# The last expert round moved into the next program block, and both halves of its down product put ahead of its spread

## The chip, the cores and the metric

The kernel runs on one core of a Trainium2 chip. The time is that of one launch in microseconds on the device, from the first to the last instruction and the little that lies around them. The core has a tensor engine (PE in the profile), a vector engine (DVE), a scalar engine (ACT), GpSimd (POOL) and SyncE (SP), which here only issues transfers. Engines run on their own instruction streams and meet through semaphores.

## What is computed

A two-layer step on 256 prompt tokens and 8 sample tokens, width 1024, all in float32. Layer 0 mixes by retention, layer 1 by gated linear attention (GLA); each is followed by a mixture of 64 experts, of which every token uses 8, plus a shared one. Cut to what matters here:

```python
for i in range(DEPTH):
    mod = silu(c) @ ada_w[i] + ada_b[i]                 # conditioning: shifts, scales, gates
    h = modulate(x, norm_mix_g[i], sh1, sc1)            # rmsnorm, scale, shift
    m, S = retention_mixer(h, ...) if i % 2 == 0 else gla_mixer(h, ...)
    x = x + g1[:, None, :] * m
    h = modulate(x, norm_ffn_g[i], sh2, sc2)
    f = moe_ffn(h, ...)      # routed: sum of w * (silu(h Wg[e]) * (h Wu[e])) Wd[e]; plus shared
    x = x + g2[:, None, :] * f
return rmsnorm(x, final_norm_g), ...
```

## The kernel before, in words

The token state is held transposed, `k.x` as 8 chunks of 128 features by 264 tokens. The kernel is a row of program blocks (`nc.Block()`): `retention`, `experts(k, 0)`, `gla`, `experts(k, 1)`, `final`. In a block each of the five engines has its own function. At the end of a block each engine drains and waits at a barrier for all five; only then does any of them start the next block.

`experts` has two blocks. In the first the 64 experts are gone through in 16 rounds of four. Weights come through a ring of 12 slots of 1 MB (`k.ring`), a round filling it once: four gate, four up, four down matrices. SP issues each load when the slot's last reader has released it (`ring_free`). Most rounds run on PE as gate and up products, the spread of the round before (`spread`: its result rows are multiplied into token columns, 8 chunks, two PSUM banks in turn), transposes of the hidden rows, the gather of the next round's rows and the down product. Each spread chunk is added on DVE to `acc` (`add_spread`, L2799).

The last two rounds, `LAST - 1` and `LAST`, are light: one tile with 32 rows for each expert. Round `LAST` in order: gate (`four_up`, L2337), spread of round `LAST - 1` (L2395), up (L2337), hidden on DVE (L2836) and its transpose (L2411), copied by ACT (L2994); the down product's first half (`four_down`, L2347), copied to `last_rows` by ACT (L3013). Meanwhile DVE adds all of `acc`, gated, to `k.x` (`add_last`, three instructions for each chunk, L2806 to L2811). `last_spread` (L2367) then spreads chunks 0 to 3 (L2380), computes the down product's second half, and spreads chunks 4 to 7. Each of these chunks goes to `k.x` by `add_last`. The down matrices of this round are loaded in halves of columns (L2252, 8 transfers of 512 KB), the first halves under a semaphore of their own.

Behind the spread, in the same block: for layer 0 the next norm (`nxt`: squares on ACT L505, sums over features on PE L524, reciprocal root, then `k.h` chunk by chunk on DVE L552 and ACT L516) and a product for the next conditioning (L457); for layer 1 the transposes back to token rows (L1912) and the final norm's sums (L1920, L1928).

The second block of `experts` holds a loop for token rows that fit in none of the 16 rounds. Every engine loads the number of such pairs (L3062, L3097 and the like) and branches over the loop when it is zero, as it is for these inputs. Then `gla` or `final` begins. The first product of `gla` (`project`, L1361) reads `k.h`, all of which is ready by the barrier; its small gate weights `a1`, `a2` are the first thing SP loads there (L1316). After the last round SP has loaded six slots for the next stage (four of conditioning weights, two of `gla_w_in`); the other slots are loaded from the next block.

## Time and profile before

| | us |
|---|---|
| median of 3 runs | 1618.62 |
| lowest, highest | 1614.11, 1620.0 |
| the profiled execution | 1614.77 |
| its span, first to last instruction | 1613.0 |
| PE busy | 1516.2 (94%) |
| DVE busy, ACT busy | 709.3 (44%), 364.3 (23%) |

The span is cut at the places of interest by instruction times counted from its start. Rows of an engine with a q behind its name (PEldq, SPq) are those of its sequencer: branches, drains, register loads, DMA issues. A number in square brackets with an arrow says how long the engine was idle before the group and what ended it. The last round of layer 0 begins near 866 us and the GLA block at 909.5 us; the last round of layer 1 begins near 1574 us and the final block at 1605.4 us.

### The profile page before, as it was taken

How to read it: one execution, taken by the hardware profiler on the slowest of the kernel's cores; microseconds unless marked ns; L12 is line 12 of the kernel's file. 1: busy time of each engine (PE TensorE's matmuls, PEld its weight loads, DVE VectorE, ACT ScalarE, POOL GpSimd, SP SyncE). 2: the span in 40 equal slices, each digit the busy share in tenths (PEclk: the TensorE clock that was granted, in tenths of full speed). 3: DMA queues.
4: the chain of work that ended last, by engine and by line, in shares of the span. 5: the costliest groups of instructions: out<-in, count | busy, mean ns of one | idle time of the engine just before them, and what ended most of it. 6: DMA issues, size and time to landing. Idle time of an engine off the chain costs nothing. (4 is left out here: it accounts for less than half of the span.)

```text
span 1613.0 us, 29632 instructions
## 1 busy us (share of the span) xinstructions
PE 1516.2 (94%) x11206; PEld 1009.5 (63%) x11206; DVE 709.3 (44%) x1980; ACT 364.3 (23%) x770; POOL 94.0 (6%) x119
## 2 busy tenths in 40 slices
PE   6999999998999999999997799999999999999986
PEld 4778765776665665565554487767566556565553
DVE  3205535215465355345454235443745534543453
ACT  3002443103111121112111244431111111211112
POOL 0000110001000000000000000001000000010000
PEclk9999999999999999999999899999999999999998
DMA  9997799339999999999999793988999999999896
GB/s 364 388 370 266 259 394 404 124 98 367 393 420 420 420 421 420 419 420 419 398 370 409 265 291 110 351 305 325 420 420 421 421 420 420 420 419 410 338 420 248
DMA packets 153578, 580.21 MB, mean 360 GB/s; under 512 B 17181, under 2 KB 62401, under 8 KB 105226
## 3 DMA queue, kind: packets, MB, share of 16 engines
q1 hardware_dynamic: 137642, 535.74, 83.8%
q0 software_dynamic: 15200, 40.92, 6.6%
q10 hardware_dynamic: 640, 2.26, 0.4%
q8 instruction: 61, 1.00, 0.3%
q14 instruction: 35, 0.29, 0.0%
HBM read 567.17 MB, written 26.90 MB: 368 GB/s over the span
## 5 line engine op out<-in xcount | busy, mean ns | idle before, releaser
L2431 PE MATMUL ps<-ring,scratch 128*64 128x256 f32 x3328 | 367.8, 380 | 10.0 <-DMA ring<-in_moe_w_up 8.8
L2431 PEld LDWEIGHTS ps<-ring,scratch 128*64 128x64 f32 x3328 | 245.0, 137 | 121.6 <-issue 14.3
L2497 PE MATMUL ps<-ring,scratch 128*64 128x512 f32 x896 | 200.5, 598 | 0.0
L698 PE MATMUL ps<-hT,ring 128*128 128x264 f32 x768 | 182.5, 392 | 1.3 <-ACT hT L380 1.3
L2836 DVE SCALAR_TENSOR_TENSOR scratch<-scratch,ps 128x256 f32<-128x256 f32 x62 | 29.8, 481 | 327.4 <-ACT scratch L2985 313.4
L2395 PE MATMUL ps<-scratch 128*128 128x264 bf16 x1392 | 169.6, 276 | 1.5 <-DVE scratch L2803 1.5
L698 PEld LDWEIGHTS ps<-hT,ring 128*128 128x128 f32 x768 | 147.6, 194 | 31.4 <-issue 2.8
L2395 PEld LDWEIGHTS ps<-scratch 128*128 128x128 bf16 x1392 | 121.8, 97 | 50.2 <-issue 14.3
L2803 DVE TENSOR_TENSOR scratch<-scratch,ps 128x264 f32<-128x264 f32 x240 | 102.6, 430 | 86.3 <-PE ps L2395 86.0
L2497 PEld LDWEIGHTS ps<-ring,scratch 128*64 128x64 f32 x896 | 58.1, 136 | 117.7 <-issue 86.2
L2985 ACT ACTIVATE scratch<-ps 128x256 f32<-128x256 f32 x62 | 23.8, 384 | 424.6 <-PE ps L2431 356.3
L2164 POOL DMA_INDIRECT scratch<-h_rows,scratch x60 | 59.8, 997 | 897.9 <-DVE scratch L2158 889.3
L3015 ACT CAST scratch<-ps 128x512 bf16<-128x512 f32 x116 | 68.0, 586 | 145.2 <-PE ps L2497 139.9
L1361 PE MATMUL ps<-hT,ring 128*128 128x264 f32 x384 | 91.9, 396 | 9.5 <-PEq L3059 9.5
L2897 DVE TENSOR_TENSOR scratch<-ps,scratch 128x512 f32<-128x512 f32 x116 | 79.7, 687 | 25.9 <-ACT scratch L3015 25.9
L1361 PEld LDWEIGHTS ps<-hT,ring 128*128 128x128 f32 x384 | 74.1, 196 | 23.4 <-issue 10.3
L2887 DVE TENSOR_TENSOR scratch<-scratch 128x512 bf16<-128x512 f32 x116 | 80.4, 693 | 4.0
L2311 PE MATMUL ps<-tab,scratch 128*128 128x128 f32 x480 | 65.1, 279 | 13.0 <-DVE scratch L2631 9.7
L2311 PEld LDWEIGHTS ps<-tab,scratch 128*128 128x128 f32 x480 | 51.8, 141 | 24.7 <-DVE scratch L2631 16.4
L955 DVE SCALAR_TENSOR_TENSOR ring<-ring,rstd 128x512 f32<-128x512 f32 x64 | 41.3, 687 | 49.7 <-ACT rstd L1108 36.7
L2631 DVE COPY scratch<-ps 128x512 f32<-128x512 f32 x60 | 41.5, 692 | 48.5 <-PE ps L2311 48.5
L859 PE MATMUL ps<-scratch,ring 128*128 128x264 f32 x256 | 57.7, 387 | 0.0
(402 smaller groups left out, 1458.3 us busy)
## 6 DMA issues: line engine op xcount, KB each, us to landing
ring<-in_moe_w_gate SPq DMA_DIRECT2D x128, 1024.0 KB, 20.1
ring<-in_moe_w_up SPq DMA_DIRECT2D x128, 1024.0 KB, 21.9
ring<-in_moe_w_down SPq DMA_DIRECT2D x120, 1024.0 KB, 18.0
ring<-in_ada_w SPq DMA_DIRECT2D x48, 1024.0 KB, 12.4
ring<-in_ret_w_in SPq DMA_DIRECT2D x24, 1024.0 KB, 16.7
ring<-in_state_ret SPq DMA_DIRECT2D x16, 1024.0 KB, 14.0
out_ret_sample<-ring POOLq DMA_DIRECT2D x16, 1024.0 KB, 9.2
ring<-in_gla_w_in SPq DMA_DIRECT2D x12, 1024.0 KB, 12.0
```

Source lines behind the costliest of these rows:

```text
L698: mm = nc.tensor.matmul(k.ps[:, bank, 0:T], w[:, c, m * P:(m + 1) * P], k.h[:, c, :], start=(c == 0), stop=(c == DC - 1))
L859: mm = nc.tensor.matmul(k.ps[:, out_bank(n), 0:T], w[:, c, m * P:(m + 1) * P], vo[:, 4 * h + c, :], start=(h == 0 and c == 0), stop=(h == ...
L1361: mm = nc.tensor.matmul(k.ps[:, bank, 0:T], w[:, c, m * P:(m + 1) * P], k.h[:, c, :], start=(c == 0), stop=(c == DC - 1))
L2164: pool.indirect_dma_start(xtok_of(p), None, h_rows[:, :], bass.IndirectOffsetOnAxis(ap=rows[:, p:p + 1], axis=0), bounds_check=ABSENT - 1, ...
L2311: mm = nc.tensor.transpose(k.ps[:, b, c * P:(c + 1) * P], xtok_of(p)[:, d0:d0 + P], ident)
L2395: mm = nc.tensor.matmul(k.ps[:, c % 2, 0:T], parts_of(p)[:, s, c * P:(c + 1) * P], slot_token[:, p, :], start=(p == 0 and s == 0), stop=(p ...
L2431: mm = nc.tensor.matmul(k.ps[lo:lo + CAP, 2 + p, j * DE:(j + 1) * DE], xg[:, p, c, lo:lo + CAP], slot(k, n, DE)[:, c, :], start=(c == 0), ...
L2497: mm = nc.tensor.matmul(k.ps[lo:lo + CAP, 6 + half, :], hid_t[:, p, m, lo:lo + CAP], slot(k, n, D)[:, m, half * 512:(half + 1) * 512], sta ...
L2803: nc.vector.tensor_tensor(acc[:, c, :], acc[:, c, :], k.ps[:, c % 2, 0:T], ALU.add).then_inc(s_add, 1)
L2887: nc.vector.tensor_tensor(parts_of(p)[:, 2, cols], rest[:, half], parts_of(p)[:, 1, cols], ALU.subtract).then_inc(s_part, 1)
L2897: nc.vector.tensor_tensor(rest[:, half], k.ps[:, 6 + half, :], parts_of(p)[:, 0, cols], ALU.subtract).then_inc(s_rest, 1)
L3015: nc.scalar.copy(parts_of(p)[:, 0, cols], k.ps[:, 6 + half, :]).then_inc(s_rhi, 1)
```

## The change

Four things are done.

1. Round `LAST` leaves the first block of `experts`. That block now ends behind round `LAST - 1`. For SP it still holds all loads of round `LAST`. At its end each engine waits for the count of extra pairs and loads it (`read_pairs`).
2. The second block is gone. `experts` returns an object with one function for each engine (`tail_tensor` and so on), and `gla` and `final` call these at the head of their own block. Each holds an `If` on the number of extra pairs, whose body has round `LAST` and the loop for the extra rows, and an `Else` with round `LAST` alone; behind both come the next norm and the conditioning product, or the final sums, and then the block's own work. What was ordered by a barrier is now ordered by semaphores: the first `project` waits for each chunk of `k.h`, `a1` is loaded when the norm's sums are done (they share memory), `final` waits for the sums.
3. In `last_spread` both halves of the down product come ahead of all eight chunks.
4. On DVE the gated addition of `acc` to `k.x` moves from round `LAST` to round `LAST - 1`, ahead of that round's hidden rows; the spread of round `LAST - 1`, done in round `LAST`, now goes to `k.x` by `add_last` and no longer to `acc`.

Beside these, SP loads all 12 slots for the next stage as they come free, and GpSimd clears old semaphores at the end of `gla` and no longer at its start.

```diff
+    def read_pairs(eng, name):
+        eng.wait_ge(s_count, 2)
+        extra_pairs[name] = eng.value_load(number, min_val=0, max_val=XPAIRS)
...
-            k.issued = n_end
-            load_until(k, sp, n_end + KEPT)
-            for i in range(KEPT):
-                sp.wait_ge(k.ring_free[(n_end + KEPT + i) % RING], (n_end + KEPT + i) // RING)
-            sp.wait_ge(s_count, 2)
-            with sp.If(sp.value_load(number, min_val=0, max_val=XPAIRS) > 0):
-                load_extra(sp, X_LOADS, pair_experts(sp, 0))
+            read_pairs(sp, "sp")
...
-        def last_spread(pe, behind):
+        def last_spread(pe, follow):
             d = done_tiles(LAST, 0)
             pe.wait_ge(s_htc, LAST + 1)
+            wait_light(pe, LAST, "moe_w_down")
+            four_down(0, LIGHT_BLOCKS, 1, LIGHT_PLACE)
             for half in range(2):
-                if half:
-                    wait_light(pe, LAST, "moe_w_down")
-                    four_down(0, LIGHT_BLOCKS, 1, LIGHT_PLACE)
-                    behind(pe, 0)
-                    behind(pe, 1)
                 pe.wait_ge(s_part, 2 * d + 1 + half)
                 for c in range(4 * half, 4 * half + 4):
                     pe.wait_ge(s_add, DC * (LAST + 1) + c - 1)
                     nc.tensor.matmul(k.ps[:, c % 2, 0:T], last_rows[:, c * P:(c + 1) * P], last_token,
                                      start=True, stop=True).then_inc(s_scat, 1)
-                    if half:
-                        behind(pe, c - 2)
+                    if c >= 2 and follow:
+                        follow(pe, c - 2)
...
-            for r in range(HEAVY - 2, LAST + 1):
+            for r in range(HEAVY - 2, LAST):
                 pe_round(pe, r)
-            last_spread(pe, x_rows if layer else nxt.sum)
...
+            read_pairs(pe, "pe")
...
+            if last:
+                for c in range(DC):
+                    v.wait_ge(s_scat, DC * (r - 1) + c + 1)
+                    add_last(v, c, k.ps[:, c % 2, 0:T], DC + c).then_inc(s_add, 1)
+            elif light(r):
+                add_spread(v, r - 1)
+                v.wait_ge(s_add, DC * (r + 1))
+                for c in range(DC):
+                    ins = add_last(v, c, acc[:, c, :], c)
+                k.dve.link(v, ins)
...
-    with nc.Block() as block:
...
+    def tail_sync(sp):
+        k.issued = n_end
+        load_until(k, sp, n_end + KEPT)
+        pairs = extra_pairs["sp"]
+        with sp.If(pairs > 0):
+            ...
+        load_until(k, sp, n_end + RING)
...
+    def tail_tensor(pe):
+        ...
+        with pe.If(pairs > 0):
+            pe_round(pe, LAST)
+            last_spread(pe, None)
+            ...
+        with pe.Else():
+            pe_round(pe, LAST)
+            last_spread(pe, follow)
+            for c in range(DC - 2, DC):
+                follow(pe, c)
+        if layer:
+            pe.wait_ge(s_final, 3)
+            final_small(k, pe, small).then_inc(s_final, 1)
+        else:
+            cond_products(k, pe, k.ps[:, 4], next_group)
...
-def gla(k):
+def gla(k, behind):
...
         @block.sync
         def _(sp):
+            behind.sync(sp)
+            sp.wait_ge(behind.norm.s_sum, 1)
             sp.dma_start(a1, inp["gla_w_a1"][0].rearrange("(c p) r -> p c r", p=P)).then_inc(s_w, 16)
...
+            behind.tensor(pe)
...
+                    if first:
+                        pe.wait_ge(behind.norm.s_h, c + 1)
...
 def final(k, behind):
...
+            behind.vector(v)
+            v.wait_ge(behind.s_sums, 2)
+            v.wait_ge(behind.s_final, 4)
```

On PE, in layer 0 where round `LAST - 1` ends with its down product (32x512), the order before goes straight on to the gate product of round `LAST` (32x256):

```order
L2347 MATMUL ps<-ring,scratch 32x512 [waits ring_full9,ring_full8,ring_full10,ring_full7,moe0_hidden_transposed_out]
L2347 MATMUL ps<-ring,scratch 32x512 x15
L2337 MATMUL ps<-ring,scratch 32x256 [waits ring_full0,ring_full1,ring_full11,ring_full2,moe0_gathered_out_odd,moe0_gathered_out_even]
L2337 MATMUL ps<-ring,scratch 32x256 x31
L2395 MATMUL ps<-scratch 128x264 [waits moe0_added,moe0_row_parts,moe0_slots_first_out]
```

In the changed kernel (its line numbers) this stands there:

```order
L2369 MATMUL ps<-ring,scratch 32x512 [waits ring_full9,ring_full8,ring_full10,ring_full7,moe0_hidden_transposed_out]
L2369 MATMUL ps<-ring,scratch 32x512 x15
L2159 TENSOR_LOAD scratch [waits moe0_listed]
L2159 ISA x2
L2252 UNCONDITIONAL_BRANCH
L1355 UNCONDITIONAL_BRANCH [waits barrier_Pool_Activation_PE_DVE_SP_release]
L3102 COMPARE_AND_BRANCH
```

A load of the count, the barrier and a branch now stand between the two rounds. The branch leads over 80 rows of the order (the `If` body) to the gate product in the `Else` body; before, the branch over the extra loop led over 48 rows.

On SP, in layer 0 where the down matrices of round `LAST` are issued in halves, the order before was:

```order
L2252 DMA ring<-in_moe_w_down 128x2x512
L300 DMA ring<-in_ada_w 128x2x1024 [waits ring_free11]
L300 DMA ring<-in_ada_w 128x2x1024 [waits ring_free0]
L300 DMA ring<-in_ada_w 128x2x1024 [waits ring_free1]
L300 DMA ring<-in_ada_w 128x2x1024 [waits ring_free2]
L300 DMA ring<-in_gla_w_in 128x8x256 [waits ring_free3]
```

In the changed kernel, at the same last half load:

```order
L2279 DMA ring<-in_moe_w_down 128x2x512
L2159 TENSOR_LOAD scratch [waits moe0_listed]
L2159 ISA x2
L2252 UNCONDITIONAL_BRANCH
L1310 UNCONDITIONAL_BRANCH [waits barrier_Pool_Activation_PE_DVE_SP_release]
L299 DMA ring<-in_ada_w 128x2x1024 [waits ring_free11]
```

SP comes to the barrier only behind the last of the eight half loads, and the loads of the next stage are behind the barrier.

On PE, in the last round of layer 0 behind the first half of the down product, the chunks of the spread (L2399) and the norm's sums (L521) now follow one another from the third chunk on:

```order
L2369 MATMUL ps<-ring,scratch 32x512 [waits ring_full9,ring_full8,ring_full10,ring_full7,moe0_slots_first_out]
L2369 MATMUL ps<-ring,scratch 32x512 x7
L2399 MATMUL ps<-scratch 128x264 [waits moe0_added,moe0_row_parts]
L2399 MATMUL ps<-scratch 128x264 [waits moe0_added] x2
L521 MATMUL ps<-scratch,tab 128x264 [waits setup_x_loaded]
L2399 MATMUL ps<-scratch 128x264 [waits moe0_added]
L521 MATMUL ps<-scratch,tab 128x264 [waits setup_x_loaded]
```

Before, four chunks stood ahead of the second half and no sum ahead of it.

## Rows read from the trace of the kernel before

**Rows 1.** Timeline, SP around the last round, layer 0: start, length, line.
```profile
861.73 15.41 SPq L2252 DMA_DIRECT2D ring<-in_moe_w_down  x8
882.34 10.51 SPq L300 DMA_DIRECT2D ring<-in_gla_w_in  x2
```
**Rows 2.** Source line L2252 in that stretch: min, median, max in ns.
```profile
L2252 SPq DMA_DIRECT2D ring<-in_moe_w_down  x8: 544/1133/4172, 861.7 to 876.1; - x8
DMA to landing us min/median/max: 11.1/15.0/17.7
```
**Rows 3.** Source lines at block ends, whole span: load of the count, branches, drain.
```profile
L3062 SPq TENSOR_LOAD <-scratch x2: 263/264/264, 904.3 to 1603.7; - x2
L2225 ACTq DRAIN  x2: 808/1114/1419, 903.3 to 1602.1; - x2
L3098 PEldq COMPARE_BRANCH  x2: 334/2028/3722, 905.4 to 1604.6; - x2
```
**Rows 4.** DMA issues from 846 to 866 us: a gather beside the weight loads.
```profile
scratch<-h_rows,scratch POOLq DMA_INDIRECT x1, 8.6
```
**Rows 5.** Timeline, PE from the last round to the GLA block, layer 0.
```profile
866.58 5.89 PE L2337 MATMUL ps<-ring,scratch 128*32 128x256 f32 x64 [5.33 <-DMA ring<-in_moe_w_gate]
876.53 3.66 PE L2337 MATMUL ps<-ring,scratch 128*32 128x256 f32 x64
881.97 1.92 PE L2347 MATMUL ps<-ring,scratch 128*32 128x512 f32 x16 [0.62 <-DMA ring<-in_moe_w_down]
884.64 1.13 PE L2380 MATMUL ps<-scratch 128*128 128x264 f32 x4 [0.74 <-issue]
886.11 1.25 PE L2380 MATMUL ps<-scratch 128*128 128x264 f32 x4 [0.35 <-DVE xT L2811]
893.12 0.61 PE L2380 MATMUL ps<-scratch 128*128 128x264 f32 x2
894.01 0.61 PE L2380 MATMUL ps<-scratch 128*128 128x264 f32 x2
909.55 10.30 PE L1361 MATMUL ps<-hT,ring 128*128 128x264 f32 x32 [9.46 <-PEq L3059]
923.45 7.39 PE L1361 MATMUL ps<-hT,ring 128*128 128x264 f32 x32
```
**Rows 6.** Timeline, DVE and ACT beside them.
```profile
896.54 0.43 DVE L541 TENSOR_SCALAR scratch<-ps 128x264 f32<-128x264 f32 x1 [1.26 <-PE ps L524]
900.52 3.30 ACT L516 ACTIVATE hT<-hT,mod 128x256 f32<-128x256 f32 x8 [3.04 <-DVE hT L552]
```
**Rows 7.** A window in the gate product: length, PE, PEld, DVE, ACT, POOL busy, clock, DMA.
```profile
868.00:870.00 2.00, 2.00 (x25) 1.02 (x21) 0.00 (x0) 0.00 (x0) 0.00 (x0) 0.50 1.04 434
```
**Rows 8.** Source line L2808, the gated addition of `acc`, from 880 to 886 us.
```profile
L2808 DVE SCALAR_TENSOR_TENSOR xT<-scratch,mod,xT x8: 475/476/480, 880.8 to 884.6; 128x256 f32<-128x256 f32 x8
```
**Rows 9.** Timeline, DVE in round `LAST - 1`, layer 0.
```profile
855.63 0.48 DVE L2836 SCALAR_TENSOR_TENSOR scratch<-scratch,ps 128x256 f32<-128x256 f32 x1 [3.27 <-PE ps L2337]
863.20 0.69 DVE L2887 TENSOR_TENSOR scratch<-scratch 128x512 bf16<-128x512 f32 x1
```
**Rows 10.** Timeline, the last round of layer 1 and the final block.
```profile
1582.38 1.71 SPq L2252 DMA_DIRECT2D ring<-in_moe_w_down  x2
1574.39 5.27 PE L2337 MATMUL ps<-ring,scratch 128*32 128x256 f32 x64 [5.96 <-DMA ring<-in_moe_w_gate]
1584.33 3.66 PE L2337 MATMUL ps<-ring,scratch 128*32 128x256 f32 x64 [0.60 <-DMA ring<-in_moe_w_up]
1589.70 1.93 PE L2347 MATMUL ps<-ring,scratch 128*32 128x512 f32 x16 [0.55 <-ACT scratch L2994]
1600.16 0.61 PE L2380 MATMUL ps<-scratch 128*128 128x264 f32 x2
1603.29 0.20 ACT L1920 ACTIVATION_READ_ACCUMULATOR scratch<-ps 128x1 f32 x1
1605.35 1.28 ACT L1945 ACT_TABLE_LOAD   x1 [1.86 <-PEq L3059]
```

More of the change, by code:

```diff
@@ L191, in build @@
         retention(k)
[L192 to L195 removed]
+        behind = experts(k, 0)
+        gla(k, behind)
+        behind = experts(k, 1)
+        final(k, behind)
 def retire_semaphores(k):
@@ L1463, in _ @@
                     pe.wait_ge(s_qk, 2 * (t - 1))
-                project(t, 0, 2 * (t % 2))
+                if t == 0:
+                    pe.wait_ge(behind.norm.s_samples, 1)
+                project(t, 0, 2 * (t % 2), first=t == 0)
                 project(t, 1, 2 * (t % 2) + 1).then_inc(k.ring_free[loads[t] % RING], 1)
@@ L1927, in final_small, with final @@
     for c in range(DC):
-        k.nc.tensor.matmul(k.ps[0:NS, 0, 0:1], small[:, c, :], k.ones[:, 0:1], start=(c == 0), stop=(c == DC - 1))
-def final(k, sums):
+        mm = k.nc.tensor.matmul(k.ps[0:NS, 0, 0:1], small[:, c, :], k.ones[:, 0:1], start=(c == 0), stop=(c == DC - 1))
+    return mm
+def final(k, behind):
     nc, out = k.nc, k.out
@@ L1937, in final @@
     meansq, root, rstd = (k.scratch[:, (TT + 1) * D + 4 * i:(TT + 1) * D + 4 * i + TT] for i in range(3))
+    sums = behind.sums
     n_gain = k.stage["final_gain"]
@@ L3025, in _ @@
             take(act, 0, 1, nc.scalar.copy, g_odd)
-            round_(0)
+            scalar_round(act, 0)
             with act.Fori(1, HEAVY - 1) as r:
-                round_(r)
-            for r in range(HEAVY - 1, LAST + 1):
-                round_(r)
-            if layer == 0:
-                for c in range(DC):
-                    act.wait_ge(s_add, DC * (LAST + 1) + c + 1)
-                    nxt.square(act, c)
-                nxt.scalar(act)
-                wait_used(k, act, next_group[-1])
-                nc.scalar.copy(next_rows(k), k.ps[:, 4, 0:256])
-            else:
-                nc.scalar.activation(silu[0:1, 0, 0:1], ident[0:1, 0:1], ACT.Sqrt)
-                act.wait_ge(s_final, 1)
-                final_squares(k, 0, sums, junk)
-                act.wait_ge(s_final, 2)
-                nc.scalar.activation(small, k.x[:, :, TP:T], ACT.Square).then_inc(s_final, 1)
-                final_squares(k, 1, sums, junk)
+                scalar_round(act, r)
+            for r in range(HEAVY - 1, LAST):
+                scalar_round(act, r)
+            read_pairs(act, "act")
     release_semaphores(k, old + routed)
@@ L3228, in experts @@
-    return sums
+        tail.s_sums, tail.s_final, tail.sums = k.sem(f"{tag}_final_sums"), s_final, sums
+    else:
+        tail.s_rows, tail.norm = k.sem(f"{tag}_next_mod_rows_out"), nxt
+    def tail_sync(sp):
[3 more added lines that the diff above has]
+        with sp.If(pairs > 0):
+            for i in range(KEPT):
+                sp.wait_ge(k.ring_free[(n_end + KEPT + i) % RING], (n_end + KEPT + i) // RING)
+            load_extra(sp, X_LOADS, pair_experts(sp, 0))
+            with sp.Fori(1, pairs) as i:
+                which_ = pair_experts(sp, i)
+                sp.wait_ge(x_gu, i)
+                load_extra(sp, X_LOADS[0:4], which_)
+                sp.wait_ge(x_dn, 2 * i)
+                load_extra(sp, X_LOADS[4:6], which_)
+            sp.wait_ge(s_final if layer else nxt.s_sum, 2 if layer else 1)
+        load_until(k, sp, n_end + RING)
```

722 lines of the change are left out of this document (356 added, 366 removed).

## The prediction

> **What bounds the kernel now.** The page gives PE 94% of the span, so a change that moves no matmul can only win or lose where PE stands still. I read it in this order. First the waits, for places where PE waits for something other than a result: the longest is 9.46 us ahead of the first GLA product, ended by the barrier behind the extra block [rows 5]. Then the timeline of PE, SP and DVE around the last expert round of each layer, since that is where the change puts its new barrier. The reader is to see two things in it. Round `LAST` of layer 0 starts at 866.58 us, held by the landing of its gate weights for 5.33 us [rows 5]. And SP is at that time in the middle of issuing the eight half loads of the down matrices: the group begins at 861.73 and ends 15.41 us later, at 877.14 [rows 1]. It isn't eight cheap issues: one takes from 0.54 to 4.17 us [rows 2], since the queue is full and SP is held until there is room. The same is seen in the next loads (two `gla_w_in` issues over 10.51 us). In layer 1 the same group ends at 1582.38 + 1.71 = 1584.09, while its gate product began at 1574.39 [rows 10]. Third, the lines at block ends, for what a barrier and a branch cost [rows 3].
>
> **The new barrier, layer 0.** All eight half loads stay in the first block, so the barrier ahead of round `LAST` can't open before 877.14. Behind it:
> - SP loads the count: 0.26 us by the row and some more for its checks and drain, 0.5 in all (an estimate; the load is the only part with a row here) -> 877.6.
> - the barrier. ACT's drain of the first block ended at 903.3 + 0.81 = 904.1 and the first load of the count began on SP at 904.3 and, as the latest, PE's branch at 905.4 [rows 3]. Taken out the load of the count, 0.5 -> 878.1. The count is loaded ahead of the barrier now.
> - PE's branch over the `If` body. One branch of this kind took 0.33 us in layer 1 and 3.72 in layer 0 [rows 3]. The new one leads further, over 80 rows of the order and not 48. I take the long one, 3.7 -> 881.8, and 0.1 to the first matmul.
>
> So the gate product starts at 881.9 and not at 866.58: **+15.3 us**. The 5.33 us that PE had waited for weights are covered by that and are no gain.
>
> In layer 0 the rule of the Trainium skill that bears on the branch is in "Runtime: NRT & Kernel Launch", section Instruction fetch mechanics: a taken branch to a place outside the pages held near the engine must first fetch them by DMA. The two branch times of rows 3 agree in kind: at one and the same line the longer is eleven times the shorter. By that rule the farther branch is the likelier to be long, in both layers; the same page gives PE the largest such memory, 2048 instructions, by which it would be short. The sum goes by the rows, and the short case is a rival below.
>
> **The rest of the round, layer 0.**
> - Gate product. PE has now idled some 19 us. It had idled 5.33 before, which already sufficed: the granted clock from 868 to 870 was 0.50, that is 1.2 GHz [rows 7], and the product took 5.89 us where the same 64 matmuls at 2.4 GHz, of the up weights, took 3.66 [rows 5]: 2.2 us lost. After 9.46 us of idling the GLA product lost 10.30 - 7.39 = 2.9 [rows 5]. I take the 2.9: **+0.7**.
> - Spread of round `LAST - 1`. Eight chunks took from 866.58 + 5.89 to 876.53, 4.1 us. DVE now needs three instructions for each chunk instead of one. The later spread shows the pace with three: a pair of chunks to the next pair 886.11 - 884.64 = 1.47 us [rows 5]. Three such steps and a last pair of 0.85 give 5.3: **+1.2**.
> - Up product to the down product: 876.53 to 881.97, 5.4 us, of which 0.62 waited for the first half of the down weights. ACT and the transposes fill the same time; I leave it at 5.4, **0**. The last half load lands at 876.1 + 11.1 = 887.2 [rows 2], long before PE is there, so neither half of the down product waits for weights.
> - Down product and spread. Before: from 881.97 to the end of the norm's sums at 896.54 [rows 6], 14.5 us, with a stop between the halves of the spread for the second half's copy and the squares queued behind it on ACT. After: two halves back to back 2 x 1.92; the first pair of chunks and its addition 1.5 (the same step of 1.47); from then on a chunk and a sum by turns at 894.01 - 893.12 = 0.89 us, five steps to the start of the last chunk; from there to the end of the sums as before, 896.54 - 894.01 = 2.5. That is 3.85 + 0.1 + 1.5 + 4.45 + 2.75 (0.2 more for a square that ACT starts later) = 12.65: **-1.9**.
>
> The sums end at 896.5 + 15.3 + 0.7 + 1.2 - 1.9 = 911.8.
>
> **The removed block ends, layer 0.** Before, from the end of the sums to the end of the first GLA product (909.55 + 10.30 = 919.85) 23.3 us passed. They were the norm, two barriers with one branch, and a product at half clock. After: the first chunk of `k.h` is out 900.52 + 0.41 + 0.1 - 896.54 = 4.5 us behind the sums [rows 6]. ACT brings one each 3.30 / 8 = 0.41 us and PE reads one in 7.39 / 16 = 0.46, so PE isn't held, and the conditioning product (3.66 us) has kept it busy until just before. 4.5 + 7.4 = 11.9: **-11.4**. Layer 0 in all: 15.3 + 0.7 + 1.2 - 1.9 - 11.4 = **+3.9 us**.
>
> **Loads of GLA.** The slots are released later (gate slots at some 888.4), but all 12 are then loaded as they come free. `a1` now stands in SP's queue behind them. Eight of the 12 MB are issued from 897.5 on, some 20 us of transfers behind the conditioning loads, so `a1` lands around 922 to 924, and it is wanted at 911.8 + 11.9 = 923.7. I take 0.5 us, with 0 and 2.6 as ends. Nothing else waits there.
>
> **The moved addition of `acc`.** In round `LAST - 1` it comes ahead of the hidden rows. Eight chunks go at (884.6 - 880.8) / 7 = 0.54 us [rows 8], 4.4 with the link; DVE idled 3.27 us there [rows 9]. PE gets its hidden rows 1.2 us later and ends the round 1.2 us later. That is covered by the wait for SP until 877.1; were that gone, it would be covered by the 5.33 us wait for weights. The down slots free 1.2 us later as well, which SP's full queue hides.
>
> **Layer 1.** SP ends at 1584.09, so the gate product starts at 1584.09 + 0.5 + 0.5 + 3.7 + 0.1 = 1588.9 instead of 1574.39 [rows 10]: +14.5. Gate: 3.66 + 2.9 = 6.6 where it took 5.27: +1.3. Spread: before it ran from 1579.7 to 1584.33, with 0.60 of waiting for the up weights that are now long there: +0.6. Down, spread, transposes: before, from 1589.70 to the start of the last chunk at 1600.16, 10.5; after 3.95 + 1.5 + 5 steps of 0.78 (the pace of this layer, four chunks in the 3.1 us to 1600.16) = 9.4: -1.0. Block end: the last sum ended at 1603.49 and the root could start at 1605.35 + 1.28 = 1606.63, behind two barriers and a table load; after, the mean square (0.4 us) and a semaphore stand between, and the order holds no table load there: 0.6 for 3.15, -2.55. In all **+12.9 us**.
>
> **The sum**: 3.9 + 0.5 + 12.9 = +17.3 us on the profiled execution's 1614.8: 1632.1. That execution lies 3.9 us below the median of the three runs (1618.6); on the median it would be 1635.9. I forecast the middle, **1634 us**.
>
> **Unknown costs.** The branch: 0.33 us at one end, which takes 3.4 from each layer. At the other end a small transfer that queued beside the weight loads, the gather [rows 4], took 8.6 us; if the code's fetch does too, each layer is 4.9 longer. On DVE and ACT the same branches are hidden by the gate product's 6.6 us. The barrier: between nothing and the 1.3 us from the end of ACT's drain to PE's branch [rows 3].
>
> **Rivals.**
> - The branch is short in both layers. For it: the 0.33 of layer 1. Against: the longer way. 1634 - 6.8 = 1627.
> - The fetch is slow beside the full queue. For it: the gather's 8.6 us, and the loads queued at 877 us land only by 887. Against: nothing shows it for code. 1634 + 9.8 = 1644.
> - `a1` behind the 12 MB costs its upper end and the conditioning loads, issued 11 us later than before, come late too: 3 to 4 us, 1638.
> - SP is not what opens the barrier, the other side: if SP handed its issues to the queue and passed on, the last to arrive would be DVE, at 863.20 + 0.69 + 1.2 = 865.1 [rows 9]. Then the gate product starts at 865.1 + 1.0 + 3.7 = 869.9, +3.3 and not +15.3, and layer 0 comes to -8.1; layer 1, at 1577.1 instead of 1574.39, to +1. Sum -7: 1610. It decides from the point where SP's group ends before DVE's round, that is at 865 instead of 877. Against it: the issue rows of up to 4.17 us, and the next SP instruction that always begins where they end.
> - The change doesn't take the block out of the path: no; the order shows one barrier fewer for each expert layer.
>
> **Chances.** Forecast 0.55, short branch 0.15, slow fetch 0.12, late loads 0.08, SP not in the way 0.10. The measurement can tell about 0.5%, 8.1 us, from no change, so slower means above 1626.7 and faster below 1610.5. Slower: all of the forecast, slow fetch and late loads, and a small half of the short branch, less a little for errors in the sum that have one sign: 0.78. Within 0.5%: 0.14. Faster: 0.08. The range for 8 in 10 is 1623 to 1645, from the short branch on the low execution to the slow fetch; the likeliest case alone spans 1630 to 1638.
>
> **What would show it.** In the new profile: SP's half loads end near 877 and the gate product of round `LAST` begins 4 to 5 us behind them, in layer 1 near 1589; PE idles there for about 19 us. PE's branch reads 3 to 4 us in both layers. Spread pairs stand 1.4 to 1.5 us apart in the round. From the first down product to the norm's sums 12.5 us. The first GLA product takes 7.4 us and follows its conditioning product within 1 us. I am wrong if the gate product starts much before SP's last half load is out, or if the GLA block doesn't win its 11 us.

## The result: 1.4% slower

| | before | after |
|---|---|---|
| median of 4 runs, us | 1617.43 | 1639.86 |
| lowest, highest | 1614.11, 1620.0 | 1636.12, 1641.77 |
| the profiled execution, its span | 1614.77, 1613.0 | 1636.12, 1634.3 |
| PE busy | 1516.2 | 1515.2 |

The ratio of after to before is 1.0137, 95% interval 1.011 to 1.0164: +22 us, from +18 to +27. The forecast was 1634 in a range of 1623 to 1645, and slower. PE's work is the same; all of the difference is PE standing still.

The profiled executions differ by a few us far ahead of the places looked at. So each stretch is measured from a point of its own: SP's issue of the gate loads of round `LAST`. In the kernel before these are the first two rows; the third is PE's last product.

```profile
846.28 1.89 SPq L2236 DMA_DIRECT2D ring<-in_moe_w_gate  x4
1553.47 2.04 SPq L2236 DMA_DIRECT2D ring<-in_moe_w_gate  x4
1602.39 0.55 PE L1928 MATMUL ps<-tab,scratch 128*8 128x1 f32 x16 [0.35 <-ACT scratch L3043]
```

After, the timeline of SP in both layers, which answers to [rows 1, 10]:

```profile
844.13 1.88 SPq L2263 DMA_DIRECT2D ring<-in_moe_w_gate  x4
862.48 12.17 SPq L2279 DMA_DIRECT2D ring<-in_moe_w_down  x8
1561.84 1.91 SPq L2263 DMA_DIRECT2D ring<-in_moe_w_gate  x4
1578.26 14.09 SPq L2279 DMA_DIRECT2D ring<-in_moe_w_down  x8
```

And what each engine's sequencer did at the new barrier (source lines L2252 and L3102: min, median, max in ns, then the first and the last start, one for each layer). It answers to [rows 3].

```profile
L2252 PEldq DRAIN  x2: 2028/2120/2213, 860.1 to 1576.0; - x2
L2252 DVEq DRAIN  x2: 95/95/95, 864.6 to 1580.7; - x2
L2252 SPq DRAIN  x2: 7/7/7, 875.3 to 1593.0; - x2
L3102 PEldq COMPARE_BRANCH  x2: 6249/6260/6272, 875.6 to 1593.3; - x2
```

PE's drain is done by 862.3, DVE's begins at 864.6, and SP comes last at 875.3, 0.65 us behind its last half load (874.65). Only then PE's branch begins, and it takes 6.26 us in both layers. In layer 1 the same is seen at 1593.

The timeline of PE in layer 0, with DVE's first step of the norm between; it answers to [rows 5, 6]:

```profile
882.24 5.68 PE L2359 MATMUL ps<-ring,scratch 128*32 128x256 f32 x64 [20.24 <-issue]
892.71 3.66 PE L2359 MATMUL ps<-ring,scratch 128*32 128x256 f32 x64
898.01 3.64 PE L2369 MATMUL ps<-ring,scratch 128*32 128x512 f32 x32 [0.46 <-ACT scratch L2875]
910.13 0.43 DVE L538 TENSOR_SCALAR scratch<-ps 128x264 f32<-128x264 f32 x1 [1.26 <-PE ps L521]
914.85 7.36 PE L1364 MATMUL ps<-hT,ring 128*128 128x264 f32 x32 [1.17 <-ACT hT L515]
927.22 5.42 PE L1474 MATMUL ps<-hT,scratch 128*16 128x264 f32 x16 [5.01 <-DMA scratch<-in_gla_w_a]
```

A stretch ahead of the gate product (20.24), one ahead of the `a1` product (5.01), and only 1.17 ahead of the first GLA product, where 9.46 us were before. The idle stretch of 20.24 says "issue": no semaphore ends it, but PE's own sequencer, which is a branch here. And in layer 1, answering to [rows 10]:

```profile
1599.95 5.23 PE L2359 MATMUL ps<-ring,scratch 128*32 128x256 f32 x64 [21.86 <-issue]
1615.26 3.64 PE L2369 MATMUL ps<-ring,scratch 128*32 128x512 f32 x32 [0.46 <-ACT scratch L2875]
1626.48 0.55 PE L1937 MATMUL ps<-tab,scratch 128*8 128x1 f32 x16 [0.35 <-ACT scratch L3261]
```

### The profile page after: what moved, and what is told of

It reads as the page before. It is cut to its first block and busy times, and to the rows that moved or that the text cites. A ratio compares the mean times of both kernels' runs of the same rounds, so it can differ in the third digit from the quotient of the medians.

```text
span 1634.3 us, 29626 instructions
## 1 busy us (share of the span) xinstructions
PE 1515.2 (93%) x11206; PEld 1006.7 (62%) x11206; DVE 713.0 (44%) x2012; ACT 363.7 (22%) x770; POOL 94.1 (6%) x119
## 3 DMA queue, kind: packets, MB, share of 16 engines
q8 instruction: 62, 1.02, 0.3%
## 5 line engine op out<-in xcount | busy, mean ns | idle before, releaser
L693 PE MATMUL ps<-hT,ring 128*128 128x264 f32 x768 | 180.8, 390 | 1.3 <-ACT hT L379 1.3
L693 PEld LDWEIGHTS ps<-hT,ring 128*128 128x128 f32 x768 | 145.7, 192 | 31.3 <-issue 2.5
L2731 DVE TENSOR_TENSOR scratch<-scratch,ps 128x264 f32<-128x264 f32 x224 | 96.5, 431 | 66.4 <-PE ps L2414 66.1
L1364 PE MATMUL ps<-hT,ring 128*128 128x264 f32 x384 | 88.9, 387 | 1.2 <-ACT hT L515 1.2
L1364 PEld LDWEIGHTS ps<-hT,ring 128*128 128x128 f32 x384 | 72.1, 190 | 14.1 <-issue 2.1
L2359 PE MATMUL ps<-ring,scratch 128*32 128x256 f32 x512 | 32.9, 414 | 42.1 <-issue 42.1
```

The lines of the kernel that those rows point to most:

```text
L693: mm = nc.tensor.matmul(k.ps[:, bank, 0:T], w[:, c, m * P:(m + 1) * P], k.h[:, c, :], start=(c == 0), stop=(c == DC - 1))
L1364: mm = nc.tensor.matmul(k.ps[:, bank, 0:T], w[:, c, m * P:(m + 1) * P], k.h[:, c, :], start=(c == 0), stop=(c == DC - 1))
L2359: mm = nc.tensor.matmul(k.ps[lo:lo + 32, bank, j * DE:(j + 1) * DE], xg_of(p)[:, c, lo:lo + 32], slot(k, n, DE)[:, c, :], start=(c == 0), ...
L2731: nc.vector.tensor_tensor(acc[:, c, :], acc[:, c, :], k.ps[:, c % 2, 0:T], ALU.add).then_inc(s_add, 1)
```

## The experiments

All times in this table are us. G is the time from the issue of the gate loads to PE's gate product; A, in layer 0, to the end of the `a1` product; Z, in layer 1, to PE's last product; "end" is from there to the end of the span. "Sum" is A + Z + end against before, which holds the places that the edits touch. Each of these columns is one profiled execution: in e5 and e12 the program of layer 0 is the same and A differs by 1.6 us, so a smaller difference between two sums needs a row that shows where it lies. The ratio is that of the timed runs with its interval.

| kernel | G, A layer 0 | G, Z layer 1 | end | sum | ratio |
|---|---|---|---|---|---|
| before | 20.30, 77.23 | 20.92, 48.92 | 10.61 | 0 | 1 |
| after | 38.11, 88.51 | 38.11, 64.64 | 7.82 | +24.2 | 1.0137 (1.011 to 1.0164) |
| e1 halves first, on before | 20.26, 76.01 | 20.83, 52.63 | 10.59 | +2.5 | 1.0056 (1.0034 to 1.0078) |
| e2 late half loads | 25.91, 83.35 | 25.75, 53.60 | 7.79 | +8.0 | 1.0065 (1.0042 to 1.0089) |
| e3 no branch | 31.76, 81.81 | 31.49, 58.14 | 7.82 | +11.0 | 1.0084 (1.0054 to 1.0115) |
| e4 hint | 38.19, 87.87 | 37.99, 65.32 | 7.86 | +24.3 | 1.017 (1.0141 to 1.02) |
| e5 late half loads, a1 early | 25.71, 70.15 | 25.79, 53.52 | 7.79 | -5.3 | 0.9981 (0.997 to 0.9991) |
| e6 e5, round ahead of the branch | 20.13, 70.98 | 21.00, 54.33 | 7.86 | -3.6 | 0.9964 (0.9952 to 0.9977) |
| e7 e6 with hint | 21.29, 70.06 | 20.88, 54.28 | 7.86 | -4.6 | 0.9981 (0.9965 to 0.9996) |
| e8 e5, no branch | 21.21, 69.20 | 21.21, 49.73 | 7.85 | -10.0 | 0.9963 (0.9949 to 0.9977) |
| e9 e6, fall through in layer 1 | 20.18, 70.99 | 21.20, 52.53 | 8.96 | -4.3 | 0.9962 (0.9948 to 0.9975) |
| e10 fall through in both | 20.21, 80.91 | 20.63, 52.40 | 7.82 | +4.4 | 1.0025 (1.0011 to 1.0039) |
| e11 short body, on after | 32.05, 82.19 | 31.77, 58.04 | 7.80 | +11.3 | 1.0063 (1.0045 to 1.0082) |
| e12 each layer its own | 27.38, 71.79 | 21.07, 50.09 | 9.03 | -5.9 | 0.996 (0.9946 to 0.9974) |

**e1: the order of the halves alone.** The kernel before with

```diff
+            wait_light(pe, LAST, "moe_w_down")
+            four_down(0, LIGHT_BLOCKS, 1, LIGHT_PLACE)
             for half in range(2):
-                if half:
-                    wait_light(pe, LAST, "moe_w_down")
-                    four_down(0, LIGHT_BLOCKS, 1, LIGHT_PLACE)
-                    behind(pe, 0)
-                    behind(pe, 1)
...
-                    if half:
+                    if c >= 2:
                         behind(pe, c - 2)
```

> The kernel before with one part of the change alone: both halves of the last down product stand ahead of the spread; the blocks stay as they were. Theory (the order gains only when the second halves have landed): in the kernel before the first half is done at 883.9 and the second halves land at about 887.2, so PE now waits there some 3.3 us in layer 0 and 3.6 in layer 1; against it stand the 1.9 and 1.0 us that the order saves. Net +1.4 and +2.3 us, about 1621, ratio 1.002, and a wait of some 3 us ended by DMA ahead of the second half. Rival (the order is worth its 2.9 us wherever the block ends stand): 1614.5, ratio 0.998.

PE's second halves in the two layers:

```profile
891.20 1.92 PE L2347 MATMUL ps<-ring,scratch 128*32 128x512 f32 x16 [3.23 <-DMA ring<-in_moe_w_down]
1596.31 3.45 PE L2347 MATMUL ps<-ring,scratch 128*32 128x512 f32 x16 [3.32 <-DMA ring<-in_moe_w_down]
```

The wait is there as expected, 3.23 and 3.32 us, and in layer 1 it also let the clock fall: the product took 3.45 for 1.92. Layer 1 got 3.7 us longer; layer 0 was 1.2 us longer up to the norm's sums, and was then made up by two things that the edit does not touch: the branch at the block's end took 2.55 us for 3.72, and the first GLA product lost less to the clock (8.90 us for 10.30). The sum of +2.5 is below the 5.5 us at the lower end of the measured interval; the rest, some 3 us or more, is not at the places of this edit, and what it is stays open. By itself part 3 of the change costs; it pays only where something has already delayed the round.

**e2: SP's half loads behind the barrier.** The changed kernel with the block of the half loads moved from the first block to the head of `tail_sync`:

```diff
             load_round(LAST, LIGHT_ROUND[:2 * EPI], LIGHT_PLACE)
-            expert_of = [expert_at(sp, LAST * EPI + e) for e in range(EPI)]
-            for half in range(2):
-                ...
     def tail_sync(sp):
+        expert_of = [expert_at(sp, LAST * EPI + e) for e in range(EPI)]
+        for half in range(2):
+            ...
```

> The changed kernel with SP's eight half loads of round LAST moved behind the new barrier. Theory (SP's held issues open the barrier): it now opens behind DVE, at 865.1 in layer 0 (was 875.5) and 1581.2 in layer 1 (was 1593.1); PE's branch keeps its 6.3 us, the gate product starts at 871.9 and 1588.0. That is -10.4 and -12; the halves are issued 3 us later and may hold the down product for 1 to 3 us in each layer, and a1 may be waited for up to 3 us longer. 1620 to 1624, ratio 1.003. Rival (another engine or the gather sets the start of the gate product): it stays near 882 and the time near 1638.

```profile
L2252 SPq DRAIN  x2: 7/7/7, 858.9 to 1571.8; - x2
L2252 DVEq DRAIN  x2: 95/95/95, 866.1 to 1579.1; - x2
L3102 PEldq COMPARE_BRANCH  x2: 6112/6173/6234, 866.6 to 1579.5; - x2
924.22 6.41 PE L1474 MATMUL ps<-hT,scratch 128*16 128x264 f32 x16 [10.15 <-DMA scratch<-in_gla_w_a]
```

SP is now through the first block 7 us ahead of DVE, and G falls by 12.2 and 12.4 us. So it was SP that held the barrier. The branch keeps its 6.1 to 6.2. The down products waited for none of the late halves, since PE was late itself. But `a1` is still the last of SP's loads, so that its wait grew from 5.01 to 10.15 us and with it more than half of layer 0's gain went: A fell by 5.2 only. The wait is 5.1 us of the difference; the rest is the clock, low for longer in the gate product (6.59 us for 5.68) and in the `a1` product (6.41 for 5.42).

**e3 and e11: the branch.** e3 leaves out the `If` and its body on all engines. e11 keeps the compare and the branch on PE but cuts the body:

```diff
         with pe.If(pairs > 0):
-            pe_round(pe, LAST)
-            last_spread(pe, None)
             pe.sem_inc(x_scat, DC)
-            pe.wait_ge(s_add, DC * (LAST + 2))
-            ...
```

> The changed kernel with the branches of the last round left out on every engine: the loop for rows beyond 64 of an expert is not in it, and the plain path stands alone; barrier and SP's loads stay. Theory (6.26 us is the jump over the body): the gate product starts 0.5 us behind the barrier's opening at 875.5, so 6 us earlier in each layer: 1627.5, ratio 1.006. a1 may give back 1 to 2 us of it in layer 0, since it still stands behind the 12 MB. Rival (PE would wait there anyway, for the fetch of whatever code comes behind the barrier, taken or not): under 1 us per layer, 1638.

> The changed kernel with PE's If body cut to one semaphore increment (the loop for rows beyond 64 of an expert is left out on PE); the compare and the branch to the plain path stay, but the path now begins some 10 instructions behind it. Theory (the price is the fetch of a far target): the row of the branch reads 0.3 to 0.6 us for 6.26 and each layer gains 5.7: 1629, ratio 1.009, as without the branch. Rival (any taken branch there costs 6 us, near or far): 1640.

PE's gate product of e3, and the branch of e11:

```profile
882.99 5.38 PE L2359 MATMUL ps<-ring,scratch 128*32 128x256 f32 x64 [13.91 <-PEq L2252]
L3102 PEldq COMPARE_BRANCH  x2: 213/222/232, 879.2 to 1590.1; - x2
```

Without the branch G fell by 6.35 and 6.62; with a near target by 6.06 and 6.34, and the branch read 0.22 us. So it isn't the compare, and not the code behind the barrier in general, but the far target. In e3 the row's reason is now the barrier (PEq L2252), where it was "issue". The Trainium skill has the mechanism ("Runtime: NRT & Kernel Launch", section Instruction fetch mechanics): the code ahead is fetched in sequence only, and a taken branch out of the two pages held must wait for a DMA. The near and the far branch agree with it; the page gives no time, and here it was 6.26 us. No run shows the fetch itself.

On DVE the same branch must be read from the instruction behind it. Here are its row and DVE's next instruction in the changed kernel, then that instruction in e3, where the barrier opened at 882.5:

```profile
L3175 DVEq COMPARE_BRANCH  x2: 63/63/63, 875.6 to 1593.2; - x2
881.30 0.20 DVE L2178 SCALAR_TENSOR_TENSOR scratch<-ps,tab 128x36 f32<-128x36 f32 x1 [16.64 <-issue]
```
```profile
882.63 0.20 DVE L2178 SCALAR_TENSOR_TENSOR scratch<-ps,tab 128x36 f32<-128x36 f32 x1 [10.90 <-PEq L2252]
```

The branch's own row reads 0.06 us, and yet DVE does nothing until 5.7 us later; without the branch it starts 0.1 us behind the barrier. In e11, which cuts PE's body only, the 5.7 us stay. In layer 1 the two stand 0.6 us apart. It costs nothing here, since DVE has only to be ready when PE's gate product ends, at 887.9.

**e4 and e7: a hint.** e4 puts it ahead of the barrier, e7 at the head of PE's tail, with the round between it and the branch:

```diff
+        names = [f"{tag}_pe_{n}" for n in ("extra", "plain", "end")]
+        pe_hint = pe.mark_branch_hint_location()
+        pe_round(pe, LAST)
+        pe.br_eq(pairs, 0, on_true=names[1], on_false=names[0]).branch_hint(pe_hint)
```

> The changed kernel with one instruction more on PE: ahead of the barrier a hint names the branch behind it and says that it will be taken. Everything is computed as before. Theory (the branch's 6.26 us are the fetch of its target's code, while SP's transfers run): fetched while PE waits for SP, the branch takes under 1 us and each layer gains some 5.5: 1629, ratio 1.007; the row of the branch shows it. Rival (the hint is lost at the two jumps between it and the branch, or the code is dropped while PE waits): the branch keeps 6 us, 1640.

> As e6_round_first, with the hint for the branch as the first instruction of PE's tail, 15 us ahead of the branch and in the same stretch of code. Theory (the hint was lost at the jumps between the blocks): the branch takes 0.3 us; with it the second half starts when its weights land, 3 us less in each layer than e6: 1600, ratio 0.991. Rival (the hint does nothing for this kind of branch, or is dropped by the code fetched on the way): the row of the branch reads 6.2 us as before and the time is that of e6.

The hint and the branch in e4, then the branch in e7 and in e6, which is e7 without it:

```profile
L2620 PEldq BRANCH_PREFETCH_HINT  x2: 40/48/55, 861.2 to 1580.7; - x2
L3104 PEldq COMPARE_BRANCH  x2: 6232/6266/6299, 878.3 to 1596.6; - x2
```
```profile
L3108 PEldq COMPARE_BRANCH  x2: 5460/5680/5901, 882.5 to 1586.2; - x2
```
```profile
L3106 PEldq COMPARE_BRANCH  x2: 5745/5770/5796, 883.4 to 1583.3; - x2
```

The hint did nothing in either place. Why is open; my guess of lost jumps between the blocks fell with e7.

**e5: a1 and a2 early.** e2 with the two small weights in columns of the scratch that the routing no longer needs, and loaded right behind the half loads (that part of the edit is left out here):

```diff
-    a1 = on_flat[:, 0:DC * RANK].rearrange("p (c r) -> p c r", c=DC)
-    a2 = on_flat[0:RANK, DC * RANK:DC * RANK + GH * GDK]
-    low = on_flat[0:RANK, 640:640 + T]
+    a1 = sc[:, 15240:15240 + DC * RANK].rearrange("p (c r) -> p c r", c=DC)
+    a2 = sc[0:RANK, 15368:15368 + GH * GDK]
+    low = sc[0:RANK, 15880:15880 + T]
```

> The changed kernel with SP's half loads behind the new barrier, as in the run before, and a1 and a2 in columns that the routing no longer needs, loaded right behind the half loads instead of behind the 12 MB. Theory (a1 was waited for since its issue stood behind full queues): the wait of 10.15 us ahead of the a1 product goes to nothing and the product runs at the full clock, 3.7 us for 6: about -12, so 1612, ratio 0.999; layer 1 stays. Rival (the two small loads, issued between, still land late or delay the weights behind them): 3 to 10 us of it come back at the next product.

```profile
878.63 1.34 SPq L1313 DMA_DIRECT2D scratch<-in_gla_w_a  x1
913.36 3.73 PE L1475 MATMUL ps<-hT,scratch 128*16 128x264 f32 x16
```

The wait is gone, the product runs at full clock, and A falls by 13.2 us. Nothing of it comes back: from the gate loads of layer 0 to those of layer 1 e5 takes 13.3 us less than e2. This kernel is the changed one without two of its three losses, and it is a little faster than the kernel before.

**e6 and e8: the branch moved, and left out.** e6 puts `pe_round(pe, LAST)` ahead of PE's `If`, so that the branch comes between the halves of the down product. e8 is e5 without the branches, as e3.

> As e5_late_a1, and PE's round LAST stands ahead of its If, so that the branch comes between the two halves of the down product. Theory (6.2 us is the fetch of the jump's target, the same wherever it stands): the gate product of layer 0 starts when its weights land, 20.3 us behind the issue of its loads, 5.5 us earlier than in e5, and the branch's 6.2 us now lie beside the wait for the second halves (3.3 us in e1): 3 us gained in each layer, 1606, ratio 0.995. Rival (nothing hides it, as the half loads come so late that they set the second half anyway): 1612.

> As e5_late_a1 with the branches of the last round left out on all engines (the loop for rows beyond 64 of an expert is not in it). Theory (what is left of the loss is PE's branch): the gate product starts at 20.3 to 21 us behind the issue of its loads, held by the barrier or by its weights, and the down product's second half waits some 3 us for the late halves: 5.5 less 3 in each layer against e5, about 1606, ratio 0.995; a rival (the halves come early enough) gives the full 5.5 in each layer: 1601.

PE's second half in layer 0 of e6, then in both layers of e8:

```profile
889.46 3.64 PE L2361 MATMUL ps<-ring,scratch 128*32 128x512 f32 x16 [4.22 <-DMA ring<-in_moe_w_down]
```
```profile
889.67 3.05 PE L2361 MATMUL ps<-ring,scratch 128*32 128x512 f32 x16 [2.85 <-DMA ring<-in_moe_w_down]
1588.05 1.92 PE L2361 MATMUL ps<-ring,scratch 128*32 128x512 f32 x16 [1.66 <-DMA ring<-in_moe_w_down]
```

The chain of work that ended last, in layer 1, has the landing of the last half load and what came behind it, in e6 and then in e8:

```profile
1576.93 11.38 DMA ring<-in_moe_w_down
1588.31 0.98 issue
```
```profile
1576.78 11.13 DMA ring<-in_moe_w_down
1587.91 0.14 issue
```

In e6 the gate product starts 5.6 and 4.8 us earlier than in e5, and nothing of it is left in A and Z. The branch is not what takes it back. It began at 883.39, while PE still computed the first half, and ended at 889.19; in layer 1 it ended at 1589.02, 0.7 us behind the landing. PE went on 0.98 us behind the landing with the branch, and 0.14 us behind it without: so the branch costs 0.8 us there and the landing of the second halves the rest of the wait, and the stop lets the clock fall too (3.64 for 1.92). Layer 0 says the same by e9 and e10, which differ there in this branch alone up to the second half: it starts 0.65 us behind the last landing with the branch taken and 0.13 without. This is the rival of e6's expectation, that the half loads come so late that they set the second half anyway. The intervals of e5, e6 and e7 overlap. e8's profile is 4.7 us better than e5's, its timed ratio 0.2% better, less than expected; it too waits for the halves, 2.85 and 1.66 us.

**e9, e10, e12: the plain path straight behind the compare.** The extra body then stands behind the plain path, and the jump over it comes last. e9 does so in layer 1, e10 in both layers; both have SP read the round's expert numbers ahead of the barrier. e12 has e5's layer 0, and in layer 1 the fall through with the spread's old order.

```diff
+            pe.br_eq(pairs, 0, on_true=names[0], on_false=names[1])
+            with nc.body(names[0], valid_engines=[pe.engine]):
+                plain()
+                finish()
+                pe.br(names[2])
+            with nc.body(names[1], valid_engines=[pe.engine]):
+                extra_rows()
+                ...
+            nc.switch_bb(names[2])
```

> As e6_round_first (the branch between the halves of the down product in layer 0), with two things more. SP reads the four expert numbers of round LAST ahead of the barrier: 4 x (0.26 + 0.15 + 0.02) = 1.7 us off the start of its half loads. And in layer 1 PE's plain path stands straight behind the compare, with the extra body behind it, so that the jump over it comes at the end of PE's work of this kernel. Theory (only a taken far branch costs 5.8 us, and at the end of layer 1 nothing waits for PE): in layer 1 the second half of the down product no longer waits 4.2 us and runs at the full clock (1.9 us for 3.6): -5.8; in layer 0 -0.3, as the branch still sets it. 1604, ratio 0.993. Rival (a compare with the far body behind it is as dear when it isn't taken, or the halves still land late): the row of the branch reads 5 us and more, or 2 us of waiting for DMA stay: 1608 to 1610.

> As e9_fall_through, with the same order in layer 0 too: the jump over the extra body now stands between the conditioning product and the first GLA product. Theory: the norm's sums end 5.9 us earlier, and the jump gives back its 5.8 us less the 1.2 us that PE idles there and what PE's sequencer runs ahead (nothing to 1.5 us), 3.1 to 4.6: -1.3 to -2.8 against e9: 1602. Rival (the jump, which depends on no comparison, is fetched ahead and costs nothing): -5.9, 1598. Rival (it costs its full 5.8 behind the k.h chunks too): 1604.

> The best of the parts, every path kept: layer 0 as e5_late_a1 (the round and the branch behind the barrier, the half loads behind it too, a1 and a2 early); layer 1 with the round ahead of its compare, the plain path straight behind it, and the old order there (the first half of the spread ahead of the second half of the down product), which fills the wait for the late halves. Theory: layer 0 as e5, 7.1 us shorter than before from the issue of the gate loads to the end of the a1 product (70.15 for 77.23); layer 1 from that issue to the last product 49.5 (48.9 before, 0.6 for the slower spread of round LAST - 1) and behind it 7.8 for 10.6: -2.2. In all -9.3: 1606, ratio 0.994. Rival (the second halves land later than 1.5 us behind the spread's first half even so, 3 to 4 us): ratio 0.996 to 0.997.

In e9, the compare that isn't taken, the jump at the end of layer 1, and layer 1's second half:

```profile
L3173 PEldq COMPARE_BRANCH  x1: 83/83/83, 1588.8 to 1588.8; - x1
L3177 PEldq COMPARE_BRANCH  x1: 3798/3798/3798, 1604.7 to 1604.7; - x1
1593.49 3.05 PE L2362 MATMUL ps<-ring,scratch 128*32 128x512 f32 x16 [2.82 <-DMA ring<-in_moe_w_down]
```

The compare costs 0.08 us where it isn't taken. But the second half still waited 2.82 us. SP began its half loads of layer 1 0.6 us earlier against the gate loads (20.93 for 21.55 us in e6) and was done no earlier (31.15 for 31.09), and the last one landed 41.25 us behind them for 41.50: the transfers were the limit, not SP. In layer 0 it began 2.6 us earlier (19.3 for 21.9) and was done no earlier either (31.6 in both). So the early numbers gained nothing, and Z came out at 52.53, not the 48.5 of the theory. In e10 the jump moved to layer 0's way:

```profile
L3177 PEldq COMPARE_BRANCH  x2: 286/2952/5618, 905.9 to 1612.3; - x2
911.69 0.46 PE L1365 MATMUL ps<-hT,ring 128*128 128x264 f32 x1 [4.33 <-ACT hT L515]
918.00 9.17 PE L1365 MATMUL ps<-hT,ring 128*128 128x264 f32 x31 [5.85 <-issue]
```

It cost its 5.62 us, ran until 911.5, and one matmul later PE stood still for another 5.85 us with nothing to wait for. I take that for the next piece of code, not yet fetched so soon behind a jump; no run here shows it apart. Against e9 layer 0 lost 9.9 us where 1 to 3 were to be gained. In e12 the old order in layer 1 did fill the wait:

```profile
1591.21 1.13 PE L2395 MATMUL ps<-scratch 128*128 128x264 f32 x4 [0.75 <-issue]
1593.81 1.93 PE L2361 MATMUL ps<-ring,scratch 128*32 128x512 f32 x16
```

Z is 50.09, 0.6 off the 49.5 of the theory, and no wait stands ahead of the second half. Layer 0 had a worse execution than e5 (A 71.79 for 70.15), and "end" was 9.03 for 7.8, as in e9, with the same rows up to the output stores: what lengthened it stays open. The median of 0.996 is the best of the kernels with every path in them, but e6, e9 and e12 can't be told apart.

## Why the prediction was right, and where it was not

The mechanism of the sum was right, the forecast case came, and its total was 4 us short: +17.3 on the profiled execution, measured +21.3 (1634.3 - 1613.0), of which -2.9 lie ahead of round `LAST` or between the layers and +24.2 in the two stretches. Point by point, the values after from the rows above:

- **SP holds the barrier: right.** Its half loads ended 30.5 us behind the gate loads, forecast 30.9 (877.14 - 846.28). e2 shows the cause: 12.3 us of each layer hang on it. The rival "SP not in the way" is out.
- **The branch: mis-sized, the largest error.** Taken 3.7 us, measured 6.26 in both layers; e3 and e11 show that it is the branch. I took the long one of [rows 3] for the price of a far branch. But the DMA engines were idle beside it, and busy beside the new one. The windows show it (length, busy times, granted clock, DMA share, GB/s), first before, then after:

```profile
905.40:909.10 3.70, 0.00 (x0) 0.00 (x0) 0.00 (x0) 0.00 (x0) 0.00 (x0) 0.50 0.03 7
1604.60:1605.00 0.40, 0.00 (x0) 0.00 (x0) 0.00 (x0) 0.00 (x0) 0.00 (x0) 1.00 0.00 0
```
```profile
875.60:881.90 6.30, 0.00 (x0) 0.00 (x0) 0.20 (x2) 0.00 (x0) 0.00 (x0) 0.50 1.04 379
```

  The rival of the slow fetch was thus right in kind and too dear: 2.6 us more for each layer, not 4.9. All other far branches of the runs agree. Those at a DMA share of 0.84 to 1.10 took 5.5 to 6.3 us (15 branches: after, e2, e4 to e7, layer 0 of e9, e10 and e12); those at 0.09 or less took 0.29 to 3.80 (the two of before, the two of e1 at the same places with 2.55 and 0.33, and at the end of layer 1 e9 3.80, e12 2.61, e10 0.29). The prediction also named the longer way, 80 rows for 48, as a reason for a dear branch. The length of the way alone doesn't do it: the two jumps of e10 lead over the same body and took 5.62 us at a share of 1.10 and 0.29 at 0.00. No run changed the DMA load alone, so this is an order among branches and not an experiment, and what spreads the idle ones from 0.29 to 3.80 stays open.
- **Start of the gate product:** forecast +15.3 and +14.5, measured +17.8 and +17.2 (38.11 for 20.30 and 20.92). The excess is the branch, nearly all of it.
- **Gate product:** forecast +0.7 and +1.3, measured -0.2 and 0.0 (5.68 for 5.89, 5.23 for 5.27). Against 3.66 us at the full clock it lost 2.0 and 1.6 us; 20 us of idling cost no more than the 5.33 us of before. My price, the 2.9 us that the GLA product had lost, was too high here. The loss doesn't grow with the idling: behind 9.4 to 9.7 us of it (e2, e5) the same product took 6.4 to 6.6 and so lost 2.8 to 2.9, more than behind 20 to 22 (1.5 to 2.4, with e4). Why is open.
- **Spread at three instructions each:** forecast +1.2, measured +0.7: from the gate product's end to the up product 4.8 us for 4.1.
- **Down products, spread and sums:** forecast -1.9, measured 910.13 - 898.01 = 12.1 for 14.6, -2.4. e1 adds what I had not asked: the gain exists only since the barrier had already delayed the round past the landing of the second halves; in the timing of before it is a loss.
- **Block ends and the GLA product, layer 0:** forecast -11.4, measured from DVE's row to the product's end 12.08 for 23.31, -11.2. Right.
- **a1: mis-sized, the second error.** Taken 0.5 us with 2.6 as the end; measured 5.01 of waiting and 1.7 for a product at the lower clock (5.42 for 3.73), +6.8. I let `a1` queue behind eight of 12 MB by bandwidth, but SP issues in order and each of the last issues ahead held it 2.8 to 3.7 us; `a1` was issued only at 917.25. It is the same held issue that I had priced for the barrier, and I did not carry it to this row. Part of the wait isn't `a1`'s own. PE waits for the count of both small loads, and the second one, `a2`, which this product doesn't read, came last:

```profile
920.22 2.84 SPq L1315 DMA_DIRECT2D scratch<-in_gla_w_a  x1
DMA to landing us min/median/max: 7.0/7.0/7.0
```

  `a1` landed 8.1 us behind its issue, at 925.3, and `a2` at 927.2. A count of its own for `a1` would have saved some 1.9 us, by these two landings; no run tried it. e2 shows that the wait was not a remainder: bring the rest forward and it doubles. The rival of late loads was right on this place and was given 3 to 4 us.
- **The moved addition of `acc`: right.** PE got the hidden rows of round `LAST - 1` 1.3 us later (a wait of 1.98 us for 0.68 before), forecast 1.2, and the wait for SP covered it.
- **Layer 1:** forecast +12.9, measured 64.64 + 7.82 - 48.92 - 10.61 = +12.9. That it fits is partly luck: the branch was 2.6 too low, and against it the gate product was 1.3 too high, the stretch behind it 1.0 and the block's end 0.2.

Layer 0 in all: forecast 4.4 with `a1`, measured 88.51 - 77.23 = +11.3; the branch with 2.5 and `a1` with 6.3 are more than the difference of 6.9, and the others together gave 1.9 back.

Added up: the later gate products cost 17.8 + 17.2 = 35.0 us and `a1` 6.8; the block ends gave back 11.2 + 2.8, and the reordered rounds 3.6. Of the 35.0 us, 24.6 went with SP's issues (e2) and 12.4 to 13.0 with the branches (e11, e3); the two together come to a little more than all, since without both the gate product waits for its weights or for DVE. Without SP's part and `a1` the changed kernel is faster than before, by 0.2% (e5).

## What to carry to other kernels

When code moves behind a barrier, look at what every engine must have issued before it, not computed: behind many open transfers each half load took SP 0.5 to 4.5 us to issue, and SP became the slowest engine of the block. Move the issues across with the code, put small transfers that are wanted soon ahead of the large ones in the same queue, and give each a count of its own where they are needed at different times. Price a jump over a large body at 6 us on PE beside full DMA queues, not at what a quiet place shows, unless PE waits there for a transfer anyway (in e6 it then cost 0.8). Read a branch's price from the start of the next instruction, as its own row can hide it (DVE). And price an order that needs a transfer earlier at nothing until the landing time has been compared with the new need.

## What the runs showed of the hardware

- A taken branch on PE: 0.22 us to a target some ten instructions on, 0.3 to 3.8 over a large body with idle DMA engines, 5.5 to 6.3 beside busy ones. Not taken 0.08 us.
- A prefetch hint on PE took 0.05 us and changed nothing in two places.
- On DVE a branch whose row reads 0.06 us was followed by 5.7 us of standing still in layer 0, 0.6 us in layer 1.
- PE's sequencer takes a branch while its products still run: in e6 it began 0.1 us behind the start of a product of 1.92 us.
- Behind a far jump of 5.62 us PE stopped once more for 5.85 us, one matmul later (e10).
- Short stops can cost the clock too. Behind 4.22 us of idling in e6 the second half ran at a granted clock of 0.50 (1.2 GHz) and took 3.64 us for 1.92, behind 2.85 us in e8 3.05 us; behind 1.66 us (e8, layer 1) and also behind 3.23 us (e1, layer 0) it ran at 1.00 and took 1.92. The window in e6:

```profile
889.50:891.50 2.00, 2.00 (x12) 0.60 (x16) 0.00 (x0) 0.00 (x0) 0.00 (x0) 0.50 1.03 416
```
